# Two-block expert kernel: where the vector engine's routing pieces and norm steps stand between the dot products of the first two expert tiles

## The reference, cut to what matters

```python
s = jnp.einsum('thpc,hpnc->thpn', q, keys)            # 8 heads, 2 halves, 128 keys
v1, i1 = lax.top_k(s[:, :, 0], 16); v2, i2 = lax.top_k(s[:, :, 1], 16)
cand = (v1[..., :, None] + v2[..., None, :]).reshape(T, 8, 256)
sc, pos = lax.top_k(cand, 16); idx = take(cidx, pos); gate = jax.nn.softmax(sc)
act = jax.nn.gelu(jnp.einsum('td,thkd->thk', xb, u_tab[idx]))
out = jnp.einsum('thk,thkd->td', gate * act, v_tab[idx])
```

## Time and profile before

| what | us |
|---|---|
| median of three runs | 2992.43 |
| the profiled execution's own time | 2995.34 |
| its span, first to last instruction | 2993.5 |
| TensorE busy (matmul) | 2684.4 (90%) |
| VectorE busy | 1895.2 (63%) |
| ScalarE busy | 1237.6 (41%) |
| GpSimd busy | 719.8 (24%) |
| gather queue (q0), share of 16 DMA engines' span | 43.6% |

### The profile page before, as it was taken

The page is one execution under the profiler, slowest core; times in us unless marked ns, Lnnn a source line. Parts: engine busy times, 40 slices in busy tenths (PEclk is TensorE's granted clock), DMA queues, the critical chain, the costliest instruction groups (busy, mean ns, idle before and its releaser), DMA issues. The chain is left out here.

```text
span 2993.5 us, 43900 instructions
## 1 busy us (share of the span) xinstructions
PE 2684.4 (90%) x16052; PEld 1821.1 (61%) x16052; DVE 1895.2 (63%) x3736; ACT 1237.6 (41%) x2740; POOL 719.8 (24%) x652
## 2 busy tenths in 40 slices
PE   8979999887787778889899899999999999899998
PEld 6668868332232333345555555699866677788876
DVE  6966568667767766986656665576666734554432
ACT  5622232344443443555555544444335355322221
POOL 0221110444454444434334344100000000100000
PEclk9989999999898999999999999999999999899998
DMA  4220032999999999999999999755421111222231
GB/s 155 67 87 4 21 108 77 397 413 404 392 401 379 412 409 415 411 406 412 420 420 410 420 419 419 306 184 180 146 78 57 64 57 60 93 96 93 84 130 48
DMA packets 128582, 714.74 MB, mean 239 GB/s; under 512 B 14232, under 2 KB 17176, under 8 KB 61720
## 3 DMA queue, kind: packets, MB, share of 16 engines
q0 software_dynamic: 73728, 536.90, 43.6%
q1 hardware_dynamic: 53528, 173.37, 16.8%
q10 hardware_dynamic: 1152, 2.10, 0.2%
HBM read 707.07 MB, written 7.86 MB: 239 GB/s over the span
## 5 line engine op out<-in xcount | busy, mean ns | idle before, releaser
L2087 POOL DMA_INDIRECT uv_rows<-in_peer_uv,expert_ids x384 | 451.1, 1175 | 462.3 <-PE expert_total L2170 270.0
L2170 PE MATMUL expert_total<-uv_rows,h 128*128 128x512 f32 x768 | 362.0, 609 | 53.2 <-ACT h L2312 53.0
L2147 PE MATMUL expert_total<-uv_rows,h 128*128 128x512 f32 x768 | 352.2, 602 | 37.1 <-ACT h L2302 37.0
L2571 DVE CUSTOM_DVE_ANT_0 uv_rows<-uv_rows,h_tok 128x1024 f32<-128x1024 f32 x192 | 234.1, 1227 | 188.3 <-DMA uv_rows<-in_peer_uv,expert_ids 188.3
L2577 DVE CUSTOM_DVE_ANT_0 uv_rows<-uv_rows,h_tok 128x1024 f32<-128x1024 f32 x192 | 232.8, 1224 | 151.9 <-DMA uv_rows<-in_peer_uv,expert_ids 150.5
L2147 PEld LDWEIGHTS expert_total<-uv_rows,h 128*128 128x128 f32 x768 | 140.2, 190 | 246.0 <-issue 145.9
L2170 PEld LDWEIGHTS expert_total<-uv_rows,h 128*128 128x128 f32 x768 | 138.4, 192 | 238.2 <-issue 122.2
L2297 ACT ACTIVATE expert_acts<-expert_dots 128x1 f32<-128x1 f32 x256 | 51.8, 202 | 326.6 <-DVE expert_dots L2571 322.5
L2147 PE MATMUL expert_total<-uv_spare,h 128*128 128x512 f32 x128 | 93.2, 870 | 100.8 <-ACT h L2302 100.7
L2308 ACT ACTIVATE expert_acts<-expert_dots 128x1 f32<-128x1 f32 x256 | 51.7, 202 | 313.8 <-DVE expert_dots L2577 313.2
L2198 PE MATMUL score_out<-ffn_half_x_hi,ffn_half_w_hi 128*128 128x256 f32 x528 | 167.7, 318 | 0.0
(11 more groups left out here) (563 smaller groups left out, 6621.9 us busy)
## 6 DMA issues: line engine op xcount, KB each, us to landing
uv_rows<-in_ffn_w_in SPq DMA_DIRECT2D x66, 512.0 KB, 7.8
ffn_in_w<-in_ffn_w_in SPq DMA_DIRECT2D x43, 512.0 KB, 3.5
mix_w<-in_w_in SPq DMA_DIRECT2D x39, 512.0 KB, 3.4
uv_spare<-in_ffn_w_in SPq DMA_DIRECT2D x22, 512.0 KB, 3.5
uv_rows<-in_ffn_w_out SPq DMA_DIRECT2D x21, 512.0 KB, 7.8
last_w<-in_ffn_w_out SPq DMA_DIRECT2D x7, 1408.0 KB, 6.5
w_in<-in_w_in SPq DMA_DIRECT2D x19, 512.0 KB, 3.5
wq_w<-in_peer_wq SPq DMA_DIRECT2D x15, 512.0 KB, 3.5
```

The costliest lines, as they stand in the source:

```text
L2087: nc.gpsimd.indirect_dma_start(out=uv[first + j].rearrange("p a d -> p (a d)"), out_offset=None, in_=uv_tab, in_offset=bass.IndirectOffset ...
L2147: mm = nc.tensor.matmul(total[:, t % 2, half], diag[:, b], v[b][:, half * T:(half + 1) * T], start=False, stop=False)
L2170: mm = nc.tensor.matmul(total[:, t % 2, half], diag[:, b], v[b][:, half * T:(half + 1) * T], start=False, stop=False)
L2571: a.tensor_tensor_reduce(out=u[b], in0=u[b], in1=h_tok[:, t], scale=1.0, scalar=0.0, op0=ALU.mult, op1=ALU.add, accum_out=dot[:, b:b + 1]) ...
```

## The change

In tiles 0 and 1 a routing piece or a norm step stands behind every four dots (after buffers 3 and 7, `BETWEEN`), and no longer one or two behind every eight. The two pieces that stood behind block 15 of the query product go behind the first dots; 12 of tile 0's pieces are then left, which take both places of rounds 0 to 5. Tile 1's 16 pieces take both places of rounds 6 to 13, and rounds 14 and 15 have none. In tile 1 the pieces keep their rounds; of two in one round the first moves behind the fourth dot. `scale_back` and `invert_next` move behind the fourth dot of their rounds, `add_back` stays behind the eighth dot of round 3, after piece 5. ScalarE's list is moved to match: the exponentials of tile 0's third group come behind the gelus of round 0, `take_scores(1)` behind those of round 5, and tile 1's exponentials behind those of rounds 8 and 12. The last `exponentials` before tile 1 still stand ahead of the tile change.

```diff
--- before.py
+++ after.py
@@ -1874,19 +1874,21 @@
 
 ROUTED_FIRST, SCORE_AFTER = 5, 2
 FIRST_PIECES = [(piece, g) for g in range(len(HEAD_GROUPS)) for piece in range(PIECES)]
-FIRST_LEFT = FIRST_PIECES[2 * (N_QUERY - ROUTED_FIRST):]
-LEFT_ROUNDS = len(FIRST_LEFT) // 2
-SECOND_AT = {LEFT_ROUNDS: (0,), LEFT_ROUNDS + 1: (1, 2), LEFT_ROUNDS + 2: (3,), LEFT_ROUNDS + 3: (4, 5), LEFT_ROUNDS + 4: (6,),
-             LEFT_ROUNDS + 5: (7, 8), LEFT_ROUNDS + 6: (9,), LEFT_ROUNDS + 7: (10, 11), LEFT_ROUNDS + 8: (12,),
-             LEFT_ROUNDS + 9: (13, 14), LEFT_ROUNDS + 10: (15,)}
+FIRST_ROUTED = 2 * (N_QUERY - 1 - ROUTED_FIRST)
+BETWEEN = (GROUPS // 2 - 1, GROUPS - 1)
+FIRST_LEFT = {divmod(n, 2): piece for n, piece in enumerate(FIRST_PIECES[FIRST_ROUTED:])}
+SECOND_FROM = len(FIRST_LEFT)
+SECOND_AT = {divmod(SECOND_FROM + n, 2): n for n in range(2 * PIECES)}
+SCORES_AT, EXPS_AT = SECOND_FROM // 2, [divmod(SECOND_FROM + 5 + half * PIECES, 2)[0] for half in range(2)]
 TURN_FIRST = 6
 BACK_TURN, BACK_ADD, BACK_SQUARE, BACK_SUM, BACK_ROOT, BACK_SCALE = 1, 3, 3, 4, 5, 6
 NEXT_SQUARE, NEXT_SUM, NEXT_ROOT, NEXT_INVERT = 7, 8, 9, 10
 
 
-THIRD_AT = {0: (0,), 1: (1, 2), 2: (3,), 3: (4, 5), 4: (6,), 5: (7, 8), 6: (9,), 7: (10, 11), 8: (12,), 9: (13, 14), 10: (15,)}
+THIRD_AT = {(0, 1): 0, (1, 0): 1, (1, 1): 2, (2, 1): 3, (3, 0): 4, (3, 1): 5, (4, 1): 6, (5, 0): 7, (5, 1): 8, (6, 1): 9,
+            (7, 0): 10, (7, 1): 11, (8, 1): 12, (9, 0): 13, (9, 1): 14, (10, 1): 15}
 SCORE_LAST = 11
-LAST_AT = {12: (0,), 13: (1,), 14: (2,), 15: (3,)}
+LAST_AT = {(12, 1): 0, (13, 1): 1, (14, 1): 2, (15, 1): 3}
 LAST_TICK = {2 + 4 * (piece - 4): (piece,) for piece in range(4, 2 * PIECES)}
 
 
@@ -2382,18 +2384,19 @@
                     exponentials(2, HEAD_GROUPS[1])
             for j in range(N_QUERY - SCORE_AFTER, N_QUERY):
                 take_first(j)
+
+            gelu(0, 0, 1)
             exponentials(3, HEAD_GROUPS[2])
-
-            gelu(0, 0, LEFT_ROUNDS - 1)
+            gelu(0, 1, SCORES_AT - 2)
             exponentials(4, HEAD_GROUPS[3])
-            gelu(0, LEFT_ROUNDS - 1, 1)
+            gelu(0, SCORES_AT - 1, 1)
             act.wait_ge(routed, 3)
             take_scores(1)
-            gelu(0, LEFT_ROUNDS, 4)
+            gelu(0, SCORES_AT, EXPS_AT[0] + 1 - SCORES_AT)
             exponentials(5, HEAD_HALVES[0])
-            gelu(0, LEFT_ROUNDS + 4, 6)
+            gelu(0, EXPS_AT[0] + 1, EXPS_AT[1] - EXPS_AT[0])
             exponentials(6, HEAD_HALVES[1])
-            gelu(0, LEFT_ROUNDS + 10, 1)
+            gelu(0, EXPS_AT[1] + 1, ROUNDS - 1 - EXPS_AT[1])
             store(0)
             act.wait_ge(routed, 5)
             take_scores(2)
@@ -2564,12 +2567,14 @@
                         dve.sem_inc(routed, 1)
                 assert n[0] == (1, 2, 4, 6, 7, 9, 12, 16)[piece], (piece, n)
 
-            def dot_round(t, r):
+            def dot_round(r, t, between):
 
                 for b in range(GROUPS):
                     dve.wait_ge(uv_in[b], (r + 1) * 16)
                     a.tensor_tensor_reduce(out=u[b], in0=u[b], in1=h_tok[:, t], scale=1.0, scalar=0.0,
                                            op0=ALU.mult, op1=ALU.add, accum_out=dot[:, b:b + 1]).then_inc(dots, 1)
+                    if b in BETWEEN:
+                        between(r % ROUNDS, BETWEEN.index(b))
 
             def dot_slot(t, at):
                 b = at % GROUPS
@@ -2671,31 +2676,37 @@
                 if SLOT <= n < SLOT + KD // 2:
                     for k in range(2 * (n - SLOT), 2 * (n - SLOT) + 2):
                         make_h2(k)
-                if n >= ROUTED_FIRST:
+                if ROUTED_FIRST <= n < N_QUERY - 1:
                     for piece, g in FIRST_PIECES[2 * (n - ROUTED_FIRST):2 * (n - ROUTED_FIRST) + 2]:
                         route(0, piece, HEAD_GROUPS[g], g)
             a.memset(zero[:, :], 0.0).then_inc(zeroed, 1)
             dve.wait_ge(h_taken, KD)
+            def between_first(r, part):
+                if (r, part) in FIRST_LEFT:
+                    piece, g = FIRST_LEFT[r, part]
+                    route(0, piece, HEAD_GROUPS[g], g)
+                if (r, part) in SECOND_AT:
+                    half, piece = divmod(SECOND_AT[r, part], PIECES)
+                    route(1, piece, HEAD_HALVES[half], len(HEAD_GROUPS) + half)
+
+            def between_second(r, part):
+                if (r, part) in THIRD_AT:
+                    half, piece = divmod(THIRD_AT[r, part], PIECES)
+                    route(2, piece, HEAD_HALVES[half], len(HEAD_GROUPS) + 2 + half)
+                if (r, part) in LAST_AT:
+                    half, piece = divmod(LAST_AT[r, part], PIECES)
+                    route(3, piece, HEAD_HALVES[half], len(HEAD_GROUPS) + 4 + half)
+                if (r, part) == (BACK_ADD, 1):
+                    add_back(0)
+                if (r, part) == (BACK_SCALE, 0):
+                    scale_back(0)
+                if (r, part) == (NEXT_INVERT, 0):
+                    invert_next(0)
+
             for r in range(ROUNDS):
-                dot_round(0, r)
-                if r < LEFT_ROUNDS:
-                    for piece, g in FIRST_LEFT[2 * r:2 * r + 2]:
-                        route(0, piece, HEAD_GROUPS[g], g)
-                else:
-                    for at in SECOND_AT[r]:
-                        route(1, at % PIECES, HEAD_HALVES[at // PIECES], len(HEAD_GROUPS) + at // PIECES)
+                dot_round(r, 0, between_first)
             for r in range(ROUNDS):
-                dot_round(1, ROUNDS + r)
-                for at in THIRD_AT.get(r, ()):
-                    route(2, at % PIECES, HEAD_HALVES[at // PIECES], len(HEAD_GROUPS) + 2 + at // PIECES)
-                for at in LAST_AT.get(r, ()):
-                    route(3, at % PIECES, HEAD_HALVES[at // PIECES], len(HEAD_GROUPS) + 4 + at // PIECES)
-                if r == BACK_ADD:
-                    add_back(0)
-                if r == BACK_SCALE:
-                    scale_back(0)
-                if r == NEXT_INVERT:
-                    invert_next(0)
+                dot_round(ROUNDS + r, 1, between_second)
             for t in range(2, TT):
                 for at in range(SLOTS):
                     dot_slot(t, at)
```

## The result

| | before | after |
|---|---|---|
| median of 20 runs each, us | 2990.14 (2982.68 to 3002.31) | 2975.72 (2966.16 to 2985.09) |
| profiled execution's own time | 2995.34 | 2973.45 |
| its span | 2993.5 | 2971.6 |
| first two tiles, from the end of the eighth gather to that of tile 1's last | 648.4 | 631.4 |
| tiles 2 and 3 | 724.5 | 725.3 |

The ratio is 0.9947 with the interval 0.9936 to 0.9957, 15.8 us of 2990; the medians are 14.4 apart. The forecast was 2971, from a median of 2992.4 before the change (three executions); 20 executions give 2990.1.

A forecast was written before the change was run, and what follows sets the result against it. The gather's DMA transfers bound the kernel, running dry when pauses broke the ring of 8 buffers. Of 30.8 us lost, 8.8 stay and 22 are won: 2992.4 becomes 2970.4, stated as 2971, range 2961 to 2992.

The forecast's parts named there:

- What stays: First two tiles with their start: of 30.8 us lost to a lower transfer rate, 8.8 were expected to remain.
- Pieces apart: VectorE's pauses in the first two tiles: single pieces end the losses, except 1.6 us behind four 5.8 us last pieces.
- that limit: Longest VectorE pause the ring of 8 buffers bears without loss, about 5.4 us, with TensorE's low clock already counted.
- Twice as many pauses: TensorE's clock in the first two tiles: more stops cost zero; mean granted clock 0.85 or more.
- The slower rival: First two tiles: TensorE's low clock at some 51 stops makes it the bound, 17 us slower, 3009; chance 0.06.
- The start: Two pieces moved from before the first dot: ninth gather 2.7 to 5.3 us earlier; of 4.9 us lost about 1 stays.
- Change of tile: From tile 0 to tile 1: TensorE's end, scores and start, then ScalarE's copies, leave 1.7 of 3.4 us lost.
- add_back: Tile 1's add_back rounds: pause falls from 7.7 to about 4.9 us; of 4.9 us lost 1.5 stay.
- Later results and scatter: First two tiles: take_scores(1) adds ScalarE work to a short pause, 1 us; scatter of single rounds, 2 us.
- Tiles 2 and 3: The following tiles, transfer-bound at 415 GB/s: same length as before, they only start earlier.
- the signs: First two tiles: 415 GB/s everywhere, mean near 417; no 10 us first-gather wait; tile 1's dots end 20 us earlier.
- half of it: First two tiles: single pauses with table loads and TensorE's turns still break the ring; 11 us won, 2981; chance 0.18.

The follow-up runs named there:

- the pairs: Kernel after with both pieces of a round put back behind the eighth dot, same pieces in the same rounds: 2992.18 us, ratio 1.0000.
- filled ones: Kernel after with zero-weight products added on TensorE before the sums behind each of the four long pauses: 2975.17 us, ratio 0.9939.
- the repeats: The kernel after, unchanged, run a second and a third time: 2970.64 and 2975.36 us, ratios 0.9931 and 0.9938.
- three of the later kernels: Kernel after with last pieces cut in two; that with add_back earlier; that with tile 2's scores earlier too: 2969.14, 2968.23, 2969.95 us.

## Why the prediction was right, and where it was not

The mechanism is shown: the pairs undo all of the gain. What stays was put at 8.8 us and is 11.2, so 19.6 are won by rate (19.2 by the times of the gathers) and not 22.

- *Pieces apart.* The direction and nearly the size were right. The term that was mis-sized is the 1.6 us for the four last pieces: by rate two of their four places lose 7.0 us in the first profile, 4.8 in the second and 2.3 in the third. The step said that a pause under 5.4 us is free and that low clock "already stands in" that limit. The limit came from the rate of one hole, with one length of low clock. Pauses made 1.2 us longer cost at most half of what it gives, and filled ones of 5.7 us cost nothing in round 10. What the filled pauses point to is how late TensorE's sums end, and not the length of the pause alone.
- *Twice as many pauses.* The clock did not fall more: 0.93 on the mean against 0.92, about 85 us at the low level in the first two tiles against 106 before. The slower rival is refuted; it priced each of some 51 stops with 6.8 us of low clock, and the trace after has 20 low stretches, 15 of them 3.4 us long. But the zero that I took isn't right everywhere: in round 10 the loss went when TensorE's sums were kept fast. The Trainium skill's rule in "TensorE: Matmul & The Clock Gate", section "HAM oscillation", of a price at each stop is half borne out: the clock fell in stops of 3.6 and 4.0 us, but in round 7 the fall delayed no dot, and in round 10 the stretch lost 1.4 to 3.8 us by rate.
- *The start.* First dot at 529.00 (forecast near 529), ninth gather at 539.77 (542 or earlier). 0.7 us stay (forecast 1) and 4.2 are won (forecast 3.9). The step was right.
- *Change of tile.* 1.8 us stay, 1.7 forecast; the repeats have 1.1 and 2.2. Half of it was given to TensorE, and the runs speak for ScalarE's copies as the larger part, so the agreement is in part luck; in three of the later kernels the same place lost 3.4, 3.2 and 2.8.
- *add_back.* 1.5 forecast and 1.5 measured, but 2.2 and 3.1 in the repeats, so the exact agreement is luck too. That the pause with add_back makes the hole is shown: alone in an empty place it loses nothing.
- *Later results and scatter.* 3 us were allowed; 0.9 are lost in the last 60 us of tile 1. No wait of GpSimd in the trace after names VectorE's routing in these tiles.
- *Tiles 2 and 3.* 725.3 us against 724.5: nothing to speak of is given back, as said.

Of the signs, the rate of 415 GB/s in all stretches failed (four moved 384 to 406, and the mean is 414, not 417), and so did the wait of under 10 us before the first gather of a round (11.3 at the longest). The dots, the start, the clock and tiles 2 and 3 came out as said: the last dot of tile 1 begins at 1176.37 instead of 1195.38. The hole shown in round 10 stands behind a pause at the eighth dot, where the long piece lies, not at the fourth.

Against a forecast gain of 22 us the ratios of the three runs of the kernel after give 15.8, 20.6 and 18.6. The two tiles with their start explain 11.2 - 8.8 = 2.4 us of what is missing; what made the first of the three the smallest isn't shown. The distance of only 4.7 us between 2971 and 2975.7 flatters the forecast: it started from 2992.4, and 22 us below the median of 20 executions, 2990.1, would be 2968. The rival "half of it" (11 us won) is about as near to 15.8 as the forecast: its reason, single pauses that break the ring, is what stayed.

## What to carry to other kernels

Where a ring of buffers feeds a transfer that is the bound, look at the longest interruption before the sum of them: here the same instructions in single pieces gave back 19 of 31 us, while 64 pauses longer by 1.2 us each cost 4.2. So spread side work until each piece is shorter than the ring's slack, and count that slack to the end of the last engine in the refill chain, at both levels of TensorE's clock. Look at the same place in several runs before a single hole is explained, and check a loss read from a transfer rate against the times at which the consumer could start: the sum repeated within 1.1 us, the holes did not.

## What the runs showed of the hardware that was not expected

- After the same stop of 3.6 us at the same place, TensorE's low clock lasted 3.4 us in four profiles and about 6.8 us in four others (and in the one with longer pauses). In these eight the 8 dots of that round took 19.9 us all the same.
- Two runs of the same code moved 421 and 395 GB/s in the same round while the dots that wait for the gathered rows kept the same times within 0.02 us.
- Eight matmuls with zero weights (3.6 us) ahead of the needed ones kept the following sums at 1.98 and 1.88 us, against 3.77 and 2.90.
- The 1071 to 1080 us of identical code behind the experts scatter by as much as a half of this change's gain.
